# Five buffers for the first modulation's weight blocks, and its first two loads issued between the rows of x

## The reference

```python
sh1, sc1, g1, sh2, sc2, g2 = modulation(cond, w_mod, b_mod)   # silu(cond) @ w_mod + b_mod, 6 x 1024
u = layer_norm(x) * (1.0 + sc1) + sh1
q, k, v, xr, gate, hy = split_projection(u, w_in)             # u @ w_in, 2816 columns
att = context_attention(q, k, v)   # latent tokens: neighbourhood_attention
rg  = rglru(xr, gate, ...)
hyo = hyena(hy, ...)               # its filters come from a small sine MLP, then Fourier transforms
mix = concatenate([att, rg, hyo]) @ w_out
x = layer_norm(ALPHA * x + g1 * mix, ln1_g, ln1_b)
u = layer_norm(x) * (1.0 + sc2) + sh2
x = layer_norm(ALPHA * x + g2 * hier_moe(u, ...), ln2_g, ln2_b)
```

## Time and profile before

| | us |
|---|---|
| median of 3 timed runs | 633.91 |
| lowest, highest | 633.49, 635.57 |
| profiled execution, its span (no other time is given for it) | 635.4 |
| PE busy | 603.2 (95%) |
| DVE busy | 440.3 (69%) |
| ACT busy | 305.8 (48%) |
| POOL busy | 187.7 (30%) |

### The profile page before, as it was taken

How to read it: one execution, slowest core, us unless ns; L and a number is a source line. 1 busy time by engine, 2 the same in 40 slices (tenths; PEclk the granted TensorE clock), 3 DMA queues, 4 the chain that set the end, 5 groups by cost and what they waited for, 6 DMA issues and landing times.

```text
span 635.4 us, 9330 instructions
## 1 busy us (share of the span) xinstructions
PE 603.2 (95%) x3353; PEld 456.4 (72%) x3353; DVE 440.3 (69%) x757; ACT 305.8 (48%) x505; POOL 187.7 (30%) x152
## 2 busy tenths in 40 slices
PE   5899999999999989998999999989999999999994
PEld 2237899999999965657988888747767677676352
DVE  3958676843995565367553499988998877883177
ACT  2649322233445453004795342846565655752354
POOL 1002233344653306141496071421212121311121
PEclk9999999999999999999999999989999999999997
DMA  8977664222312259774871706769999999999787
GB/s 291 372 248 284 247 180 156 101 100 67 133 66 68 92 198 325 302 281 101 292 248 69 277 23 232 276 147 374 379 376 408 397 380 400 366 383 379 267 306 146
DMA packets 40127, 154.63 MB, mean 243 GB/s; under 512 B 7103, under 2 KB 17215, under 8 KB 27538
## 3 DMA queue, kind: packets, MB, share of 16 engines
q1 hardware_dynamic: 27912, 115.41, 50.1%
q10 hardware_dynamic: 5610, 23.21, 9.5%
q0 software_dynamic: 6560, 15.42, 8.3%
HBM read 141.32 MB, written 23.63 MB: 260 GB/s over the span
## 4 chain that ended last, share of the span: by engine, by line
PE 74%; DVE 12%; DMA 9%; issue 2%; ACT 2%; POOL 0%; DVEq 0%; ACTq 0%; POOLq 0%; SPq 0%
PE bank L1576 12%; PE bank L1577 12%; PE bank L1900 11%; PE bank L1772 9%; PE bank L1954 7%; DMA arena<-in_w_mod 3%; PE bank L1749 3%; PE bank L1412 2%; DMA arena<-in_moe_w_gu 2%; PE bank L1479 2%; PE bank L1882 2%; PE bank L1627 2%; PE bank L1676 2%; PE bank L1732 2%; DVE gate_up_low L2546 1%
## 5 line engine op out<-in xcount | busy, mean ns | idle before, releaser
L773 POOL TENSOR_TENSOR w_low<-arena,w_high 128x1024 fp32r<-128x1024 f32 x22 | 53.5, 2432 | 149.6 <-ACT w_high L974 149.6
L2546 DVE TENSOR_TENSOR gate_up_low<-arena,gate_up_high 128x1024 fp32r<-128x1024 f32 x64 | 75.3, 1221 | 13.9 <-ACT gate_up_high L1258 11.9
L1258 ACT ACTIVATE gate_up_high<-arena 128x1024 fp32r<-128x1024 f32 x64 | 63.9, 1053 | 17.9 <-DMA arena<-in_moe_w_gu 17.6
L974 ACT ACTIVATE w_high<-arena 128x1024 fp32r<-128x1024 f32 x22 | 23.2, 1058 | 88.2 <-PE bank L1577 87.3
L1576 PE MATMUL bank<-u_high,w_high 128*128 128x320 f32 x176 | 56.3, 320 | 1.9 <-DVE u_low L2159 1.9
L1954 PE MATMUL bank<-arena 128*128 128x512 f32 x128 | 57.7, 593 | 0.0
L1577 PE MATMUL bank<-u_high,w_low 128*128 128x320 f32 x176 | 54.4, 309 | 0.0
L1576 PE MATMUL bank<-u_low,w_high 128*128 128x320 f32 x176 | 54.4, 309 | 0.0
L1576 PE MATMUL bank<-u_high,w_low 128*128 128x320 f32 x176 | 54.4, 309 | 0.0
L1577 PE MATMUL bank<-u_low,w_high 128*128 128x320 f32 x176 | 54.4, 309 | 0.0
L1577 PE MATMUL bank<-u_high,w_high 128*128 128x320 f32 x176 | 54.4, 309 | 0.0
(11 more groups left out here) (441 smaller groups left out, 1400.1 us busy)
## 6 DMA issues: line engine op xcount, KB each, us to landing
arena<-in_moe_w_gu SPq DMA_DIRECT2D x38, 1024.0 KB, 11.9
arena<-in_w_mod SPq DMA_DIRECT2D x24, 1024.0 KB, 6.8
arena<-in_moe_w_down ACTq DMA_DIRECT2D x13, 1024.0 KB
arena<-in_w_in SPq DMA_DIRECT2D x11, 1024.0 KB, 4.8
arena<-in_moe_w_down SPq DMA_DIRECT2D x6, 1024.0 KB
y_scr<-arena SPq DMA_DIRECT2D x11, 512.0 KB, 9.3
arena<-in_x SPq DMA_DIRECT2D x10, 512.0 KB, 7.4
arena<-y_scr SPq DMA_DIRECT2D x10, 512.0 KB, 5.8
```

What stands on the lines that cost most here:

```text
L773: G.tensor_tensor(WL[s_][:, :, w], ring[s_][:, :, w], WH[m % 2].bitcast(F), ALU.subtract).then_inc(wl_rdy, 1)
L974: S.activation(WH[m % 2], ring[(m // 2) % 2][:, :, (m % 2) * P:(m % 2 + 1) * P], ACT.Copy).then_inc(wh_rdy, 1)
L1258: S.activation(WGH[j][c], raw_gu[s][:, c, :, :], ACT.Copy).then_inc(wgh_rdy, 1)
L2546: tt_(WGL[s][c], raw_gu[s][:, c, :, :], WGH[j][c].bitcast(F), ALU.subtract).then_inc(wgl_rdy, 1)
```

## The change

- The blocks of the first modulation rotate through five buffers: the three of before, `flat[2]` (the ring's third part, where w_high comes later) and `flat[0]`. A block waits for a product from k = 5 on, not from k = 3 on.
- The two added buffers signal on `win_in`, the semaphores of w_in's pieces, so that every count on these rises by one transfer, and the counts of the second modulation on `mod_in` are adapted.
- Blocks 0 and 1 are issued behind tiles 1 and 3 of x.
- Piece 0 of w_in waits for mod1(4), which reads its buffer; piece 1 waits for mod1(7) in place of mod1(5).

```diff
-        mod1_buf = [arena[:, MTAT:MTAT + 2048], arena[:, MTAT + 2048:MTAT + 4096], flat[1]]
+        mod1_buf = [arena[:, MTAT:MTAT + 2048], arena[:, MTAT + 2048:MTAT + 4096], flat[1], flat[2], flat[0]]
+        mod1_in = mod_in + win_in
...
-            eng.wait_ge(win_in[p % 2], 16 * (p // 2 + 1))
+            eng.wait_ge(win_in[p % 2], 16 * (p // 2 + 2))
...
             eng.dma_start(consts, t["consts"]).then_inc(ld_const, 16)
-            for i in range(TT):
-                eng.dma_start(X[:, i, :], t["x"][i * P:(i + 1) * P, :]).then_inc(ld_x[i], 16)
...
             def mod1_block(k):
-                if k >= 3:
-                    eng.wait_ge(mod1_mm, k - 2)
-                eng.dma_start(mod1_buf[k % 3], t["w_mod"][k * P:(k + 1) * P, 0:2048]).then_inc(mod_in[k % 3], 16)
+                if k >= 5:
+                    eng.wait_ge(mod1_mm, k - 4)
+                eng.dma_start(mod1_buf[k % 5], t["w_mod"][k * P:(k + 1) * P, 0:2048]).then_inc(mod1_in[k % 5], 16)
 
             def w_in_piece(p):
-                if p == 1:
-                    eng.wait_ge(mod1_mm, 6)
+                if p < 2:
+                    eng.wait_ge(mod1_mm, 8 if p else 5)
...
-            for k in range(KT):
+            def x_rows(i):
+                eng.dma_start(X[:, i, :], t["x"][i * P:(i + 1) * P, :]).then_inc(ld_x[i], 16)
+
+            for i in range(TT):
+                x_rows(i)
+                if i in (1, 3):
+                    mod1_block(i // 2)
+            for k in range(2, KT):
                 mod1_block(k)
...
-                eng.wait_ge(mod_in[k % 3], 16 * (k // 3 + 1))
-                mod_block(B[4], k, mod1_buf[k % 3]).then_inc(mod1_mm, 1)
+                eng.wait_ge(mod1_in[k % 5], 16 * (k // 5 + 1))
+                mod_block(B[4], k, mod1_buf[k % 5]).then_inc(mod1_mm, 1)
...
-                eng.wait_ge(mod_in[b % 3], 16 * ((3, 3, 2)[b % 3] + b // 3 + 1))
+                eng.wait_ge(mod_in[b % 3], 16 * (3 + b // 3))
```

## The result

| | median us | executions | ratio to before (95%) |
|---|---|---|---|
| before | 635.17 (633.49 to 639.23) | 11 | |
| changed | 638.87 (636.5 to 642.52) | 11 | 1.0052 (1.0033 to 1.0072) |

The account below looks back on a forecast made before the run. DVE was taken to bound the start up to 28.9 us, then PE. Stall +1.3, early projection piece -0.1 and buffers 0 gave +1.2 us: 635.1 from the median, 636.6 profiled; range 633.0 to 637.0.

Parts of the forecast that it names:

- What bounds the kernel: Start of kernel: DVE bounds until 28.9 us, then PE without gaps; w_mod blocks already in time, five buffers gain almost nothing.
- Part 2: Blocks 0 and 1 ahead of x's tile 4: it lands at about 23.8 us, DVE stalls from 22.48, +1.3 us.
- Tile 3 hid: x's tile 3, behind block 0 only, lands at 19.9 us before DVE asks at 21.08; no cost.
- Rival A: Tile 4 of x is not late for DVE; 0 - 0.1, 633.8 us; chance 0.12.
- Part 3: Projection's first two w_in pieces: earlier piece 0 ends ACT's 0.9 us wait, gaining 0.1 us; later piece 1 costs 0.
- D: Projection stage: the early w_in piece gains its full 0.8 us; +0.5 in all, 634.4 us; chance 0.07.
- PE's clock: PE's low clock near 31 to 35 us taken as unchanged despite the 1.3 us longer gap; at most +0.4 us.
- C: Clock falls at both PE gaps or returns after 38 us, costing a further 1.7; +2.9, 636.8 us; chance 0.15.
- B: PE's low clock stretch moves forward over idle time, ending near 31 us; -0.1, 633.8 us; chance 0.10.

Follow-up runs that it names:

- five_x_first: Changed kernel with five buffers kept but all five tiles of x issued ahead of block 0; ratio 1.0010 to the kernel before.
- three_between: Kernel before, still with three buffers, but blocks 0 and 1 issued between x's tiles; ratio 1.0075 to the kernel before.
- after_filled: Changed kernel with an unread product in PE's first gap and bank 6's product moved into the second; ratio 1.0015 to the kernel before.
- after_again: The changed kernel run again unedited; ratio 1.0079 to the kernel before.
- before_dve_longer: Kernel before with DVE taking tile 4's moments twice, 1.4 us longer, no transfer moved; ratio 1.0070 to the kernel before.
- block1_last: Changed kernel with block 0 still between x's tiles but block 1 issued behind tile 4; ratio 1.0018 to the kernel before.
- before_moments: Kernel before with DVE's moments of tile 4 moved behind the first two filter parts; ratio 0.9970 to the kernel before.
- before_again: The kernel before run again unedited; ratio 0.9999 to the kernel before.
- after_moments: Changed kernel with DVE's moments of tile 4 moved behind the first two filter parts; ratio 0.9983 to the kernel before.

## Why the prediction was wrong, by its steps

**What bounds the kernel: right.** PE had no wait for w_mod to lose. The single wait named after the DMA became one more of "issue", and five_x_first, which keeps all that the five buffers could give, is at 1.0010.

**Part 2, the stall on tile 4: right in cause, of the right size.** Forecast 1.3 us; the traces of the changed kernel (two), three_between and after_filled show 0.83, 1.51, 0.83 and 1.79. Tile 4 landed at 22.9 to 23.5 us, by the set of bytes ahead of it (forecast 23.8), while DVE came to it between 21.1 and 22.6. Tile 3 hid, as said. The Trainium skill's rule that an engine's part of the increment comes behind its earlier writes (DMA: Bandwidth & Descriptors, section Queues, rings and completion order) fits: in these four traces tile 4 landed 0.8 to 1.2 us after the queue had moved the 5.0 MB by the sum over all engines. Rival A is out.

**Part 3, w_in's early piece: right.** ACT no longer waits, and POOL's overlap with the first u_low is gone; all eight u_low of the kernel after took the short time:

```profile
L2165 DVE TENSOR_TENSOR u_low<-arena,u_high x8: 824/825/826, 55.7 to 68.5; 128x640 fp32r<-128x640 f32 x8
```

(durations in ns: least, median, most; 1709 was the most in the earlier trace rows.) PE's first projection product came at 56.63, 0.17 us later than before instead of 1.05, and at the stage's end 69.33 against 68.39 + 1.05 = 69.44 left 0.1 of it. D is out.

**PE's clock: this step failed.** The sum took it as unchanged, up to +0.4, and gave C a chance of 0.15, on the ground that "today the one gap was followed by one low stretch". That was read off a single execution, and it was one of the dearer ones: the kernel before usually has a mean clock of 0.993 to 0.994, and its second trace has no low stretch here. What the change does is make low clock more frequent and longer: in the trace of after_again a stretch of 10 us at the lower level, 3.8 us lost on PE where the sum had at most 0.4. On average over executions the clock's share is 1.5 to 3.2 us, by the reckoning under after_filled. C had the cause right, the longer idle of PE ahead of 30 us. Where the low time lay it had only in part: it put a second stretch on the work behind 35 us, while in after_again and three_between one long stretch began near 27 us, behind the new gap, and ended near 38. Its price of 1.7 us lies at the lower end of what was measured. B is out: where the low stretch began at the new gap it did not end near 31 us, and in the first trace of the changed kernel it began at 32. The Trainium skill's remark that short idles between matmul groups can make the clock go down and up (TensorE: Matmul & The Clock Gate, section A second HAM failure mode: psum-queue depth-cycling) agrees in its direction with the mean clock of 0.987 against 0.994, and deserved more weight than one trace that showed a single fall.

**The base.** The forecast's absolute time also stood on three runs with a median 1.3 us under that of eleven; that is luck of the draw and no part of the mechanism.

## What to carry to other kernels

Where an engine takes its inputs in a fixed order, a transfer that goes ahead of them is paid by the first instruction whose cover it eats; add up the bytes ahead of that input before and after. One to two microseconds of new idle on TensorE cost another 1.5 to 3.2 through the clock here, so price a new gap also with the slow durations of the groups behind it, and try filling it with products that are due anyway. One profile shows one draw of the clock: ask for the mean clock of several executions before calling it unchanged.

## What the runs showed of the hardware

- Four traces have two unfilled gaps on TensorE between 24 and 30 us: a first one of 1.2 to 1.9 us, and the second ahead of the last filter group (1.37 us at full clock). Two had the lower clock for about 10 us from 27 us on (after_again, three_between), one for some 3.5 us from 32 us on (the first of the changed kernel), and one not at all in this stretch (before_dve_longer).
- Six traces have the gap of 1.37 us and at most 0.23 us ahead of the products that DVE's first filter part releases. Three had a low stretch behind it (before and block1_last some 3.5 us, before_moments 7), three had none (before_again, five_x_first, after_moments).
- The four traces in which a product was moved into the second gap, so that 0.32 us of it were left, had a full clock from 27 to 38 us, after_filled too, with 1.09 us in its first gap.
- The eleven executions of the changed kernel spread over 6 us (636.5 to 642.5).
- At the lower clock four filter products took 3.78 us against 1.98, eight of mod1 1.93 against 1.06.
- With the same bytes ahead of it, tile 4 took 18.7 to 19.2 us to land in four traces (two of the changed kernel, three_between, after_filled) and came at 22.9 to 23.5 us; with one block fewer ahead of it (block1_last) DVE had it by 22.4. The place where DVE came to it varied by more (21.1 to 22.6 us).
